# Slabs behind a norm that run unscaled, two-head units in window attention, and modulation rows spread over two layers

## The chip, the cores and the metric

The kernel runs on one core of a Trainium2 chip. The metric is the time of one execution on the device in microseconds (us), all weights read from HBM. The engines are TensorE (PE, its weight loads PEld), VectorE (DVE), ScalarE (ACT), GpSimd (POOL) and SyncE (SP, here only DMA issues). They run their own instruction streams and wait for each other on semaphores.

## What is computed

Two blocks in a row on one sequence of 512 tokens of width 1024, everything in float32. Cut to what matters:

```python
# first block
n = rms_norm(h, attn_norm_w); proj = n @ w_in
y_attn = windowed_gqa_sink(rope(norm(aq)), rope(norm(ak)), av, sink)  # 8 heads, |i-j| <= 128, sink logit in the softmax
y_ret  = silu(rg) * rms_norm(bidirectional_retention(rope(rq), rope(rk), rv))
h = h + concat(y_attn, y_ret) @ w_out
m = rms_norm(h, ffn_norm_w); h = h + (silu(m @ w_gate) * (m @ w_up)) @ w_down
# second block: nine modulation vectors of 1024 from c
mod = silu(c) @ w_ada + b_ada      # sh1 sc1 g1 sh2 sc2 g2 sh3 sc3 g3
u = rms_norm(x) * (1 + sc1) + sh1; x = x + 0.5 * g1 * swiglu(u)
u = rms_norm(x) * (1 + sc2) + sh2; z = u @ w_mix + b_mix   # mLSTM, forgetting attention, gates
x = x + g2 * (merged @ w_out)
u = rms_norm(x) * (1 + sc3) + sh3; x = x + 0.5 * g3 * swiglu(u)
```

## The kernel before

Activations lie transposed: `h`, `xh`, `xl` are 128 partitions by 8 chunks of 512 tokens. A float32 product is made of three matmuls in the reduced type fp32r: high part by high part, high by low and low by high (`slab`, L384). The unit of work is a **slab**: the weights of one output tile of 128 columns, eight blocks of 128x128, so 24 matmuls of 128x512; in a down-projection two slabs of eleven blocks (33 matmuls) make a tile. Slabs are numbered through the program. Slab n is loaded by SP into `raw` (L274, once the `w_lo` of slab n-2 is there), ACT copies it to the high part `whi` (L776, once PE is done with slab n-2), POOL subtracts for the low part `wlo` (L338), and PE runs it. There are two buffers at each place.

The stages in slabs: `att` 6, `ret` 16 in four **mixing steps**, `out` 8, `ff0` 44, `down0` 16, `ff1` 44, `down1` 16, `mlstm` 24, `fox` 24, `merge` 32, `out2` 8, `ff2` 44, `down2` 16. The scheduling is written out by hand in the order of each engine's program.

**Norms.** There are five, r = 0 to 4. While a stage ends, ACT squares each finished chunk of `h` (L804) and DVE adds it to `ssum` (L1250). PE then sums over partitions (`norm_sum`, L395), ACT makes `rstd` by Ln and Exp (L808, L810), DVE scales the chunk by weight and `rstd` (L1263), ACT makes `xh` (L820 to L828), and the low part `xl` comes from DVE for even chunks (L1269) and from POOL for odd ones (L345, `norm_lows`). PE's first slab takes chunk by chunk what is ready.

**Mixing steps.** Each step t does two heads of window attention as eight units of one head and one block of 128 queries: `win_scores` (L436 and L437 are the query-key product, L439 and L441 the masks), the maximum and Exp on DVE and ACT, DVE's scaling (L1414), `win_turn` (L451, transposes of `prob`), `win_values` (L463). Between the units stand pieces of the four `ret` slabs, and at the end the retention of two heads (L480 to L520). ACT moves the ret tiles out of PSUM (`ret_tile` and others). The sink enters by an Exp of its own on ACT (L869) and an addition on DVE (L1410).

**Modulation.** 72 rows of `w_ada` (`adaw`, 128x1024 each) are multiplied by `crow` and summed on DVE (L1534), all beside `ff0`: nine steps of four slabs with eight rows each. In a step DVE makes for each of two tiles the product (`aprod`, L1520), two rows, the low part (L1526), two rows. `adaw` has two buffers.

**Gates.** Behind norm 3 PE first makes the 96 gate rows (L599), and a chain on ACT, DVE, PE and POOL's and ACT's queues leads from them (`zg`, L1013) to the slabs of the mLSTM.

## Time and profile before

| | us |
|---|---|
| median of three runs | 2174.14 (2173.87 to 2176.86) |
| the profiled execution | 2177.48 |
| its span | 2175.7 |
| PE busy | 2048.2 |
| DVE, ACT, POOL busy | 879.9, 771.4, 794.7 |
| the five norms' sums: PE waits for `ssum` | 30.6 |

The span runs from the first instruction to the last; the execution is 1.8 longer. A busy time is the time in which the engine had an instruction under way. The rows that follow further down come from a list of what PE waited for, from the timeline (one row for a group of equal instructions in a row: start, duration, engine, line, operation, what is written and read, count, and in brackets the idle time before and who ended it) and from windows (a stretch of the span with each engine's busy time in it).

### The profile page before, as it was taken

Reading aid. Unit: us, or ns where it says so; the run is one execution under the profiler, and the core shown is the slowest. Engines: PE = TensorE matmul, PEld = TensorE weight load, DVE = VectorE, ACT = ScalarE, POOL = GpSimd, SP = SyncE. Lnnn points to the kernel's source line nnn. Section 1 sums busy time; section 2 is a strip of 40 time slices with the busy share of each in tenths; the row PEclk is TensorE's granted clock in tenths of the full one; section 3 lists DMA queues with packets and bytes.
Section 4 is the critical chain, followed back from the end, with each engine's and each line's share of the span. In section 5 each row is a group of like instructions: output and inputs, shape, how many; then the busy total and the mean of one; then the engine's idle time right before and its main releaser. Section 6 shows DMA issues by size and latency. Waiting matters only on the chain.

```text
span 2175.7 us, 27408 instructions
## 1 busy us (share of the span) xinstructions
PE 2048.2 (94%) x9306; PEld 1603.5 (74%) x9306; DVE 879.9 (40%) x1215; ACT 771.4 (35%) x1197; POOL 794.7 (37%) x322
## 2 busy tenths in 40 slices
PE   5988898888899899999989999999999998999999
PEld 3666676677778778888866776677688886888887
DVE  6556555555542232222236555444421244222200
ACT  4433333222222242222225455555532224222221
POOL 3211134333344344444433233122234444444443
PEclk9999999999999989999999999999999998999999
DMA  4111113777632223333221122111123332333332
GB/s 132 58 39 39 39 58 126 241 233 237 232 126 93 91 68 96 96 96 109 93 79 53 63 67 68 49 51 55 59 78 96 96 97 68 96 96 96 107 101 92
DMA packets 56630, 210.57 MB, mean 97 GB/s; under 512 B 6288, under 2 KB 7056, under 8 KB 56592
## 3 DMA queue, kind: packets, MB, share of 16 engines
q1 hardware_dynamic: 55440, 208.71, 30.1%
q10 hardware_dynamic: 1152, 1.38, 0.2%
q8 instruction: 21, 0.34, 0.1%
q14 instruction: 17, 0.14, 0.0%
HBM read 207.96 MB, written 2.10 MB: 97 GB/s over the span
## 4 chain that ended last, share of the span: by engine, by line
PE 69%; issue 15%; DMA 7%; DVE 4%; POOL 2%; ACT 2%; DVEq 0%; ACTq 0%; SPq 0%; POOLq 0%
PE bank L384 62%; DMA adaw<-ada_dram 7%; POOL wlo L338 2%; DVE adaw L1534 2%; PE bank L617 1%; PE bank L672 1%; PE bank L687 1%; PE bank L698 1%; PE bank L707 1%; DVE sqn L1263 1%; DVE ssum L1250 1%; POOL xl L345 1%; DVE xl L1269 0%; PE bank L395 0%; PE bank L408 0%
## 5 line engine op out<-in xcount | busy, mean ns | idle before, releaser
L338 POOL TENSOR_TENSOR wlo<-raw,whi 128x1024 fp32r<-128x1024 f32 (+1 forms) x298 | 762.7, 2560 | 1320.9 <-ACT whi L776 1320.9
L384 PE MATMUL bank<-xh,whi 128*128 128x512 f32 x1744 | 715.3, 410 | 54.4 <-DVE aprod L1520 25.9
L384 PE MATMUL bank<-xh,wlo 128*128 128x512 f32 x1744 | 689.9, 396 | 0.0
L384 PE MATMUL bank<-xl,whi 128*128 128x512 f32 x1744 | 689.4, 395 | 0.0
L776 ACT ACTIVATE whi<-raw 128x1024 fp32r<-128x1024 f32 (+1 forms) x298 | 330.4, 1109 | 655.9 <-PE bank L384 624.8
L384 PEld LDWEIGHTS bank<-xh,whi 128*128 128x128 f32 x1744 | 334.1, 192 | 150.9 <-issue 68.8
L384 PEld LDWEIGHTS bank<-xl,whi 128*128 128x128 f32 x1744 | 334.9, 192 | 72.2 <-issue 7.4
L384 PEld LDWEIGHTS bank<-xh,wlo 128*128 128x128 f32 x1744 | 333.4, 191 | 72.1
L384 PE MATMUL bank<-acth,whi 128*128 128x512 f32 x528 | 205.6, 389 | 0.1
L384 PE MATMUL bank<-actl,whi 128*128 128x512 f32 x528 | 205.4, 389 | 0.0
L384 PE MATMUL bank<-acth,wlo 128*128 128x512 f32 x528 | 205.4, 389 | 0.0
L1520 DVE TENSOR_TENSOR aprod<-bank,gsil 128x512 f32<-128x512 f32 x66 | 45.5, 689 | 335.7 <-PE bank L384 335.7
L1534 DVE SCALAR_TENSOR_TENSOR adaw<-adaw,crow 128x1024 f32<-128x1024 f32 x72 | 114.7, 1602 | 103.3 <-DMA adaw<-ada_dram 103.3
L1526 DVE TENSOR_TENSOR actl<-aprod,acth 128x512 f32 x66 | 123.1, 1865 | 45.6 <-ACT acth L993 45.6
L384 PEld LDWEIGHTS bank<-acth,whi 128*128 128x128 f32 x528 | 99.1, 188 | 21.7 <-issue 1.2
L384 PEld LDWEIGHTS bank<-acth,wlo 128*128 128x128 f32 x528 | 99.1, 188 | 20.7
L384 PEld LDWEIGHTS bank<-actl,whi 128*128 128x128 f32 x528 | 99.1, 188 | 20.4
L1250 DVE TENSOR_TENSOR ssum<-ssum,sqn 128x512 f32<-128x512 f32 x40 | 93.3, 2334 | 36.2 <-ACT sqn L804 35.5
L988 ACT ACTIVATE gsil<-bank 128x512 f32<-128x512 f32 x66 | 39.1, 593 | 173.1 <-PE bank L384 173.0
L1502 DVE SCALAR_TENSOR_TENSOR h<-bank,gat,h 128x512 f32 x24 | 18.0, 751 | 199.8 <-PE bank L384 199.8
L1396 DVE TENSOR_REDUCE stat<-bank 128x1 f32<-128x256 f32 (+3 forms) x96 | 47.1, 491 | 118.1 <-PE bank L679 64.8
L993 ACT ACTIVATE acth<-aprod 128x512 f32 (+1 forms) x66 | 41.6, 630 | 102.5 <-DVE aprod L1520 102.5
(287 smaller groups left out, 1871.9 us busy)
## 6 DMA issues: line engine op xcount, KB each, us to landing
raw<-w_dram SPq DMA_DIRECT2D x250, 512.0 KB, 3.6
adaw<-ada_dram SPq DMA_DIRECT2D x72, 512.0 KB, 4.2
raw<-wd_dram SPq DMA_DIRECT2D x48, 704.0 KB, 4.0
h<-x_dram SPq DMA_DIRECT2D x4, 512.0 KB, 5.7
out_dram<-h SPq DMA_DIRECT2D x8, 256.0 KB, 4.3
rel<-rel_dram ACTq DMA_DIRECT2D x1, 513.0 KB, 5.0
crow<-c_dram SPq DMA_DIRECT2D x1, 512.0 KB, 3.3
gates_raw<-gates_dram SPq DMA_DIRECT2D x1, 384.0 KB, 8.8
```

The lines of the kernel that those rows point to most:

```text
L338: nc.gpsimd.tensor_tensor(wlo[:, s, 0:width], raw[:, s, 0:width], whi[:, s, 0:width].bitcast(F32), ALU.subtract).then_inc(sem("w_lo"), 1)
L345: nc.gpsimd.tensor_tensor(xl[:, c, :], tmp[c % 3], xh[:, c, :].bitcast(F32), ALU.subtract).then_inc(sem("x_lo1"), 1)
L384: mm = nc.tensor.matmul(proj[b][:], w[:, s, W], v[:, k, :], start=first and j == 0 and a == 0, stop=last and j == len(chunks) - 1 and a == ...
L617: mm = nc.tensor.matmul(bank[5 + j][:, b * P:S], w, sT[:, b % 2, 0:S - b * P], start=b == 0, stop=b == NB - 1, skip_group_check=True)
L776: nc.scalar.activation(whi[:, s, 0:width], raw[:, s, 0:width], ACT.Copy).then_inc(sem("w_hi"), 1)
L988: nc.scalar.activation(gsil[:, jj, :], proj[0][:], ACT.Silu).then_inc(sem("evac0"), 1)
L993: nc.scalar.activation(chunk(acth, j), aprod[:, jj, :], ACT.Copy).then_inc(sem("act_hi"), 1)
L1250: V.tensor_tensor(ssum[:], ssum[:], sqn[:, k, :], ALU.add).then_inc(sem("ssum"), 1)
L1396: V.tensor_reduce(st[:, 0:1], bank[2 + k % 2][:, 0:width], AX.X, ALU.max).then_inc(sem("rowmax"), 1)
L1520: V.tensor_tensor(aprod[:, jj, :], proj[1][:], gsil[:, jj, :], ALU.mult).then_inc(sem("evac1"), 1)
L1526: V.tensor_tensor(chunk(actl, j), aprod[:, jj, :], chunk(acth, j).bitcast(F32), ALU.subtract).then_inc(sem("act_lo"), 1)
L1534: V.scalar_tensor_tensor(W, W, 1.0, crow[:], ALU.mult, ALU.mult, accum_out=modc[:, bass.ds(v * KC + k, 1)]).then_inc(sem("ada_acc"), 1)
```

## The change

1. *Norms.* In the step before a norm, ACT also writes the chunk times the norm's weight, without `rstd`, to `xh` (`z_high`) and DVE its low part to `xl` (`z_low`). The first two slabs behind norms 1, 2 and 4, and the first slab and the gates behind norm 3, run on these; `norm_sum` stands before the fourth chunk of the first of them. The result is multiplied by `rstd` on leaving PSUM (`ff_first`, `gates_scaled`). For r of 2 to 4 the shift is added through two matmuls of 128x2 per chunk (`shs`) and a small sum on DVE (`shift_column`). Chunk by chunk, as the second of the two frees them, `xh` and `xl` are written properly scaled for all further slabs. POOL now makes two of the low parts, chunks 1 and 3, with a `wlo` behind each. Behind norm 0 all of `att` and `ret` runs unscaled, and DVE takes the factor in when it moves a tile out of PSUM (`att_scaled`, `ret_tile`; this was ACT's).
2. *Start.* SP loads the columns, weights and input in another order; ACT issues the constants' loads after the sixth chunk.
3. *Window attention.* Units of two heads: the query-key product in F32 with the two heads in the two halves of the rows (L498), the sink as one more column by a matmul with one column (L505), the values of both heads in turns (L528). DVE no longer splits queries and keys. Its order in a step is changed; `ret_queries` stands ahead of the second rope.
4. *Modulation rows.* Four per step: 28 beside `ff0` (7 steps), 44 beside `ff1` (11 steps). SP issues the rows of a step beside the weights of the step after it, those of the last step in a loop of their own ahead of `down1`.

```diff
+            def load_x(c):
+                sp.dma_start(h[:, c * 2 * S:(c + 1) * 2 * S], x_in[:, c * 2 * S:(c + 1) * 2 * S]).then_inc(sem(f"x_in{c}"), 16)
+
+            sp.dma_start(col[:], cols_in).then_inc(sem("cols_in"), 16)
+            load_wide(None, 2, 0, 0)
+            load_x(0)
+            load_x(1)
+            load_wide(None, 2, 0, 1)
+            load_x(2)
+            load_x(3)
             sp.dma_start(gates_raw[:], gates_in).then_inc(sem("gates_in"), 16)
...
+            def load_ada(i, r0, s):
+                sp.wait_ge(sem("ada_acc"), primed(i * 4 + (r0 + max(s - 1, 0))))
+                sp.dma_start(adaw[:, s % 2, :], ada_in[bass.ds(i * 4 + (r0 + s), 1)].rearrange("a p n -> (a p) n")
+                             ).then_inc(sem(f"ada_in{s % 2}"), 16)
+
+            with sp.Fori(0, ADA0) as i:
                 for s in range(4):
                     load_wide(i, 4, SLAB["ff0"] + 4, s)
-                    for k in range(2 * s, 2 * s + 2):
-
-                        sp.wait_ge(sem("ada_acc"), primed(i * KC + max(k - 1, 0)))
-                        sp.dma_start(adaw[:, k % 2, :], ada_in[bass.ds(i * KC + k, 1)].rearrange("a p n -> (a p) n")
-                                     ).then_inc(sem(f"ada_in{k % 2}"), 16)
-            wide_loop(SLAB["ff0"] + 4 * (NMOD + 1), (N_FF - 4 * (NMOD + 1)) // 2)
+                    load_ada(i, 0, s)
+            wide_loop(SLAB["ff0"] + 4 * (ADA0 + 1), (N_FF - 4 * (ADA0 + 1)) // 2)
             down_loop(0)
-            wide_loop(SLAB["ff1"], N_FF // 2)
+            for s in range(4):
+                load_wide(None, 4, SLAB["ff1"], s)
+            with sp.Fori(0, FC // 2 - 1) as i:
+                for s in range(4):
+                    load_wide(i, 4, SLAB["ff1"] + 4, s)
+                    load_ada(i, 4 * ADA0, s)
+            with sp.Fori(0, 1) as i:
+                for s in range(4):
+                    load_ada(i, 4 * ADA0 + 4 * (FC // 2 - 1), s)
             down_loop(1)
...
             def norm_lows(r):
 
-                for c in range(1, KC, 2):
-                    pool.wait_ge(sem("x_hi"), KC * r + c + 1)
-                    nc.gpsimd.tensor_tensor(xl[:, c, :], tmp[c % 3], xh[:, c, :].bitcast(F32),
-                                            ALU.subtract).then_inc(sem("x_lo1"), 1)
-
-
-            low_loop(0, 2, WC)
-            norm_lows(0)
-            low_loop(2, SLAB["ff0"], WC)
+                n = SLAB[FIRST[r]] + 2
+                norm_low(r, 1)
+                low(n, 0)
+                norm_low(r, 3)
+                low(n + 1, 1)
...
-                nc.tensor.matmul(bank[4][:], ones[:], ssum[:], start=True, stop=True).then_inc(sem("norm_sum"), 1)
+                nc.tensor.matmul(bank[6][:], ones[:], ssum[:], start=True, stop=True).then_inc(sem("norm_sum"), 1)
+
+            def unscaled(r, hi, lo, dst, at, j, done, rows=P):
+
+                for k in range(KC):
+                    if j == 0:
+                        pe.wait_ge(sem("z_lo"), primed(KC * r + k + 1))
+                        if k == 3:
+                            norm_sum(r)
+                            if r > 1:
+                                pe.wait_ge(sem("shifts"), r - 1)
+                    if r > 1:
+                        for a, w in enumerate((hi, lo)):
+                            nc.tensor.matmul(bank[5][0:rows, at:at + 2], w(k), shs[:, r - 2, k, :], start=k == 0 and a == 0,
+                                             stop=k == KC - 1 and a == 1, skip_group_check=True)
+                    for a, (w, v) in enumerate(((hi, xh), (hi, xl), (lo, xh))):
+                        mm = nc.tensor.matmul(dst, w(k), v[:, k, :], start=k == 0 and a == 0, stop=k == KC - 1 and a == 2,
+                                              skip_group_check=True)
+                    if k == KC - 1:
+                        mm.then_inc(sem(done), 1)
+                    elif j == 1:
+                        mm.then_inc(sem("z_used"), 1)
...
+            def win_scores(t, b):
+
                 lo, hi = keys(b)
-                H = slice(e * DH, e * DH + DH)
-                if k == 0:
-                    pe.wait_ge(sem("q_low"), t * 2 + 2)
-                if k >= 2:
-                    pe.wait_ge(sem("probs"), t * 8 + (k - 1))
-                elif not isinstance(t, int) or t > 0:
-                    pe.wait_ge(sem("ret_decayed"), t * 2 + (k - 1))
-                dst = bank[2 + k % 2]
-                W = window(k)
-                B, C = slice(b * P, (b + 1) * P), slice(lo * P, (hi + 1) * P)
-
-                nc.tensor.matmul(dst[:, 0:W], wqs[:, e, B], wks[:, e, C], start=True, stop=False, skip_group_check=True)
-                mm = nc.tensor.matmul(dst[:, 0:W], wqs[H, e, B], wkl[H, C], start=False, stop=False, skip_group_check=True)
+                W = window(2 * b)
                 if b > 0:
-                    mm = nc.tensor.matmul(dst[:, 0:P], identb[:], geb[:], start=False, stop=b == NB - 1, skip_group_check=True)
-                if b < NB - 1:
-                    mm = nc.tensor.matmul(dst[:, W - P:W], identb[:], leb[:], start=False, stop=True, skip_group_check=True)
-                mm.then_inc(sem("scores"), 1)
+                    pe.wait_ge(sem("probs"), t * 8 + 2 * b)
+                elif t == 0:
+                    pe.wait_ge(sem("rope_out"), primed(2))
+                else:
+                    pe.wait_ge(sem("ret_decayed"), t * 2)
+                C = slice(lo * P, (hi + 1) * P)
+                for e in range(2):
+                    H = slice(e * DH, e * DH + DH)
+                    nc.tensor.matmul(bank[2 + e][:, 0:W], qall[H, t, b * P:(b + 1) * P], kf[H, C], start=True, stop=False, skip_group_check=True)
+                for e in range(2):
+                    dst = bank[2 + e]
+                    if b > 0:
+                        nc.tensor.matmul(dst[:, 0:P], identb[:], geb[:], start=False, stop=b == NB - 1, skip_group_check=True)
+                    if b < NB - 1:
+                        nc.tensor.matmul(dst[:, W - P:W], identb[:], leb[:], start=False, stop=True, skip_group_check=True)
+                    nc.tensor.matmul(dst[:, W:W + 1], ident[:], c1("sink", t + e * (AH // 2)), start=True, stop=True,
+                                     skip_group_check=True).then_inc(sem("scores"), 1)
...
+                for b in range(NB):
+                    win_turn(t, 2 * b)
+                    win_turn(t, 2 * b + 1)
+                    if b + 1 < NB:
+                        win_scores(t, b + 1)
+                    if b == 1:
+                        wide("ret", t, 4, 1, part=(0, 3))
+                        ret_turn(t, 0)
+                        wide("ret", t, 4, 1, part=(3, 6))
+                    else:
+                        for j, lo, hi in RET_BESIDE[b]:
+                            wide("ret", t, 4, j, part=(lo, hi))
+                    if b == 2:
+                        ret_turn(t, 1)
+                    win_values(t, b)
...
+            def ff_tiles(run):
+                for j in range(2):
+                    unscaled_slab(NORM[run], j, bank[2 + j][:], 2 * j, j)
+                for s in range(2, 4):
+                    ff_slab(run, 0, s)
...
+            def z_high(r, m, weight):
+
+                nc.scalar.activation(chunk(xh, m), chunk(h, m), ACT.Identity, scale=weight(m)).then_inc(sem("z_hi"), 1)
+
+            def norm(r, shift=None, splits={}):
+
+                inverse_root("norm", r, bank[6][:], rstd[:], D)
+                    if c in splits:
+                        split(0, 2, SLAB[FIRST[r]] + 2, splits[c], WC)
...
+            def z_low(r, m, weight):
+
+                dve.wait_ge(sem("z_hi"), m + (KC * r + 1))
+                V.scalar_tensor_tensor(chunk(xl, m), chunk(h, m), weight(m), chunk(xh, m).bitcast(F32), ALU.mult,
+                                       ALU.subtract).then_inc(sem("z_lo"), 1)
...
-                for c in range(0, KC, 2):
-                    low(c)
-                    for d in (c + 3, c + 4):
-                        if d < KC:
-                            scaled(d)
+                low(0)
+                scaled(3)
+                scaled(4)
+                low(2)
+                scaled(5)
+                low(4)
+                if beside:
+                    beside()
+                scaled(6)
+                low(5)
+                scaled(7)
+                low(6)
+                low(7)
...
+            def ret_tile(t, j):
+                matmuls(t * 4 + (SLAB["ret"] + j + 1))
+                if j < 2:
+                    V.scalar_tensor_tensor(rraw[:, j, :], proj[j][:], DH ** -0.5 if j else 1.0, rstd[:], ALU.mult,
+                                           ALU.mult).then_inc(sem(f"evac{j}"), 1)
+                else:
+                    V.tensor_tensor((vraw, rsil)[j - 2][:], proj[j - 2][:], rstd[:], ALU.mult).then_inc(sem(f"evac{j - 2}"), 1)
...
+            def ff_first(run):
+                n = SLAB[f"ff{run}"]
+                matmuls(n + 1)
+                V.tensor_tensor(aprod[:, 1, :], bank[2][:], rstd[:], ALU.mult).then_inc(sem("evac0"), 1)
+                if run > 0:
+                    shift_column(0, 0)
+                matmuls(n + 2)
+                V.tensor_tensor(aprod[:, 0, :], bank[3][:], rstd[:], ALU.mult).then_inc(sem("evac1"), 1)
+                if run > 0:
+                    shift_column(2, 1)
+                    dve.wait_ge(sem("z_bias"), (0, 2, 6)[run])
+                dve.wait_ge(sem("evac1"), primed(TILE[f"ff{run}"] // 2 + 1))
+                dve.wait_ge(sem("ff_sil"), run + 1)
+                V.scalar_tensor_tensor(aprod[:, 0, :], aprod[:, 0, :], fb[:, 1:2] if run > 0 else 0.0, gsil[:, 0, :], ALU.add,
+                                       ALU.mult).then_inc(sem("ff_first"), 1)
...
+            def ff_beside_ada(run, i, r0, i0):
 
                 for jj in range(2):
-                    ff_product(0, i, i0, jj)
-                    ada_parts(v, range(4 * jj, 4 * jj + 2))
-                    ff_low(0, i, i0, jj)
-                    ada_parts(v, range(4 * jj + 2, 4 * jj + 4))
+                    if i0 or jj:
+                        ff_product(run, i, i0, jj)
+                    else:
+                        ff_first(run)
+                    ada_part(i, r0, 2 * jj)
+                    ff_low(run, i, i0, jj)
+                    ada_part(i, r0, 2 * jj + 1)
...```

How it moves instructions, at the three places that matter most. PE's stream at the start of `ff1` (`xh`, `xl` activations, `shs` the shift, `z_lo` and `x_lo0`, `x_lo1` the semaphores of low parts), before:

```order
L384 MATMUL bank<-acth,wlo 128x512
L398 REGISTER_ALU
L398 COMPARE_AND_BRANCH
L395 MATMUL bank<-ssum,ones 128x512 [waits ssum]
L589 UNCONDITIONAL_BRANCH
L589 ISA
L375 ISA [waits w_lo]
L384 MATMUL bank<-xh,whi 128x512 [waits x_lo0,evac0]
L384 MATMUL bank<-xl,whi 128x512
```

and after, from the third chunk of the first slab on:

```order
L447 MATMUL bank<-shs,whi 128x2 [waits z_lo]
L447 MATMUL bank<-shs,wlo 128x2
L450 MATMUL bank<-xh,whi 128x512
L450 MATMUL bank<-xl,whi 128x512
L450 MATMUL bank<-xh,wlo 128x512
L434 MATMUL bank<-ssum,ones 128x512 [waits ssum,z_lo]
L447 MATMUL bank<-shs,whi 128x2 [waits shifts]
L447 MATMUL bank<-shs,wlo 128x2
L450 MATMUL bank<-xh,whi 128x512
```

The sum has moved from ahead of the slab to its fourth chunk, and two small matmuls stand ahead of each three. POOL's stream at the same norm, before:

```order
L345 TENSOR_TENSOR xl<-sqn,xh 128x512 [waits x_hi] x2
L345 TENSOR_TENSOR xl<-ssum,xh 128x512 [waits x_hi]
L345 TENSOR_TENSOR xl<-sqn,xh 128x512 [waits x_hi]
L334 UNCONDITIONAL_BRANCH
L334 ISA
L338 TENSOR_TENSOR wlo<-raw,whi 128x1024 [waits w_hi]
```

and after:

```order
L379 TENSOR_TENSOR xl<-sqn,xh 128x512 [waits x_hi]
L373 TENSOR_TENSOR wlo<-raw,whi 128x1024 [waits w_hi]
L379 TENSOR_TENSOR xl<-sqn,xh 128x512 [waits x_hi]
L373 TENSOR_TENSOR wlo<-raw,whi 128x1024 [waits w_hi]
L364 UNCONDITIONAL_BRANCH
```

Two weights' low parts have moved between and behind the two activations' that are left. SP's stream at the end of `ff1`, before:

```order
L274 ISA [waits w_lo]
L274 DMA raw<-w_dram 128x1024
L285 REGISTER_ALU
L285 COMPARE_AND_BRANCH
L291 UNCONDITIONAL_BRANCH
L291 ISA
L274 ISA [waits w_lo]
L274 DMA raw<-wd_dram 128x1408
```

and after:

```order
L286 DMA raw<-w_dram 128x1024
L330 REGISTER_ALU
L331 ISA [waits ada_acc]
L331 DMA adaw<-ada_dram 128x1024
L342 REGISTER_ALU
L342 COMPARE_AND_BRANCH
L346 UNCONDITIONAL_BRANCH
L331 DMA adaw<-ada_dram 128x1024 [waits ada_acc] x4
L346 REGISTER_ALU
L346 COMPARE_AND_BRANCH
L303 UNCONDITIONAL_BRANCH
L303 ISA
```

Four rows of `adaw`, each with a wait for DVE's products, now stand between the last slab of `ff1` and the first of `down1`.

## Rows read from the trace of the kernel before

**Rows 1.** The page, busy us, share of the span, instructions.

```profile
PE 2048.2 (94%) x9306; PEld 1603.5 (74%) x9306; DVE 879.9 (40%) x1215; ACT 771.4 (35%) x1197; POOL 794.7 (37%) x322
```

**Rows 2.** Windows: stretch, length, busy PE PEld DVE ACT POOL, clock, DMA share, GB/s.

```profile
73.78:128.77 54.99, 49.12 (x262) 34.50 (x263) 33.53 (x73) 21.38 (x51) 12.19 (x5) 0.94 0.16 48
...
338.80:359.10 20.30, 10.87 (x28) 6.01 (x28) 13.85 (x14) 11.41 (x15) 8.58 (x5) 0.75 0.22 77
359.10:633.60 274.50, 248.43 (x1033) 198.98 (x1032) 144.09 (x186) 67.84 (x87) 109.15 (x43) 0.96 0.66 219
...
753.40:775.30 21.90, 12.38 (x28) 7.31 (x28) 13.55 (x14) 13.49 (x18) 8.75 (x5) 0.61 0.08 24
775.30:1009.40 234.10, 234.06 (x1033) 193.51 (x1032) 62.53 (x42) 68.83 (x86) 103.77 (x43) 1.00 0.31 96
```

**Rows 3.** What PE waited for: us in total, times, longest.

```profile
PE bank L395 <- DVE ssum L1250: 30.6, 5, 13.9
PE bank L384 <- DVE aprod L1520: 25.9, 12, 3.5
...
PE bank L451 <- DVE prob L1414: 6.9, 8, 1.1
PE bank L499 <- DVE kz L1346: 6.3, 4, 1.7
```

**Rows 4.** Timeline at norm 2.

```profile
754.80 2.34 POOL L338 TENSOR_TENSOR wlo<-raw,whi 128x1024 fp32r<-128x1024 f32 x1 [5.08 <-ACT whi L776]
...
755.28 2.41 DVE L1250 TENSOR_TENSOR ssum<-ssum,sqn 128x512 f32<-128x512 f32 x1 [0.85 <-ACT sqn L804]
757.74 2.07 PE L395 MATMUL bank<-ssum,ones 128*128 128x512 f32 x2 [4.17 <-DVE ssum L1250]
...
764.12 0.77 PE L384 MATMUL bank<-xh,whi 128*128 128x512 f32 x1 [4.31 <-DVE xl L1269]
```

**Rows 5.** Timeline at the start.

```profile
7.48 6.26 DVE L1250 TENSOR_TENSOR ssum<-ssum,sqn 128x512 f32<-128x512 f32 x8 [5.08 <-ACT sqn L804]
...
24.41 0.77 PE L384 MATMUL bank<-xh,whi 128*128 128x512 f32 x1 [8.47 <-DVE xl L1269]
...
34.72 0.40 PE L384 MATMUL bank<-xh,whi 128*128 128x512 f32 x1
```

**Rows 6.** Timeline, small matmuls of the mixing steps and of the forgetting attention.

```profile
82.17 0.87 PE L463 MATMUL bank<-pT,vtok 128*64 128x128 f32 x6
...
93.99 0.42 PE L436 MATMUL bank<-wks,wqs 128*128 128x384 f32 x1
...
94.72 0.23 PE L439 MATMUL bank<-geb,identb 128*128 128x128 bf16 x1
...
107.25 0.66 PE L480 MATMUL bank<-ident,rkf 128*128 128x128 f32 x4
...
1429.04 0.92 PE L672 MATMUL bank<-fk,fq 64*128 64x384 f32 x4
1429.50 0.64 PE L676 MATMUL bank<-fsp,selp 64*128 64x384 f32 x2
...
1443.91 0.88 PE L698 MATMUL bank<-fpT,fv 128*64 128x128 f32 x12
```

**Rows 7.** Timeline from the gates to the second slab of the mLSTM.

```profile
1151.08 0.69 ACT L1013 ACTIVATE zg<-bank,col 96x512 f32<-96x512 f32 x1 [2.60 <-PE bank L599]
...
1170.13 0.80 PE L384 MATMUL bank<-xh,whi 128*128 128x512 f32 x1 [2.77 <-POOL wlo L338]
```

**Rows 8.** The page's DMA issues, groups by form, and one load in ff0.

```profile
raw<-wd_dram SPq DMA_DIRECT2D x48, 704.0 KB, 4.0
...
L776 ACT ACTIVATE whi<-raw 128x1408 fp32r<-128x1408 f32 x48 | 66.3, 1382 | 260.1 <-PE bank L384 260.1
...
L338 POOL TENSOR_TENSOR wlo<-raw,whi 128x1408 fp32r<-128x1408 f32 x48 | 154.5, 3220 | 196.5 <-ACT whi L776 196.5
...
368.45 0.33 SPq L274 DMA_DIRECT2D raw<-w_dram  x1
```

More of the change, by code:

```diff
@@ L164, in build @@
         ry = sb("ry", [P, S], F32, abs_)
-        kf = ry
+        kf = sb("kf", [P, S], F32, abs_)
         abs_.close()
@@ L653, in mlstm_head @@
                 wide("mlstm", hd, 6, 7, part=(6, KC))
-            for s in range(2):
-                wide("mlstm", 0, 6, s)
+            slab(SLAB["mlstm"] + 1, 1, 1, (TILE["mlstm"] + 1) // 2, xh, xl, range(KC), ready=("x_lo", 3))
             with pe.Fori(0, MH) as hd:
@@ new lines, in _ @@
+            FF_SPLITS = {0: 0, KC - 1: 1}
+            steps("out", 2, N_OUT // 2, out_step(1, "out", scale_of(1)), "ff0")
+            norm(1, splits=FF_SPLITS)
+            ff_steps(0, "down0")
+            steps("down0", 4, N_DOWN // 4, down_step(2, "down0", scale_of(2)), "ff1")
+            norm(2, shift=0, splits=FF_SPLITS)
+            ff_steps(1, "down1")
+            steps("down1", 4, N_DOWN // 4, down_step(3, "down1", scale_of(3)), "mlstm")
+            norm(3, shift=3, splits={0: 0})
```

476 lines of the change are left out of this document (255 added, 221 removed).

## The prediction

> **What bounds the kernel now.** I read the page's totals first. TensorE is busy for 94% of the span [rows 1], so a gain must be a stretch in which PE waits, runs slowly, or does work it need not do. The windows by stage come next [rows 2]. The stretch 775.3 to 1009.4 is the second feed-forward layer behind its first slab: 43 slabs in 234.1 us, 5.44 us each, at granted clock 1.00. The stretch 359.1 to 633.6 is the same work in the first layer, 43 slabs in 274.5 us, with DMA at 219 GB/s. The two stretches around a norm (338.8 and 753.4) hold one slab each and last 20.3 and 21.9 us. One mixing step lasts 54.99 us, of which PE is busy 49.12. Third, the list of PE's waits [rows 3]: `ssum` (the norms' sum of squares) 30.6 us, `aprod` 25.9, `prob` 6.9, `kz` 6.3. So there are three costs that a change can take: the norms, the modulation rows beside the first layer, and the mixing steps. One execution gives all durations: 2177.5 us, 3.3 above the median of the runs, 2174.1. I sum against the first and take 3.3 off.
>
> **Modulation rows, +40.4.** Eight rows per step of four slabs make 8 x 0.5 MB plus 4 x 0.5 MB in about 25.6 us; DVE then gets the rows late, `aprod` late, PE waits. The whole loss is the difference of the two rows of [rows 2]: 274.5 - 234.1 = 40.4, waits of 25.9 and slowed matmuls (clock 0.96) together. Four rows per step need 4 MB in 21.8 us, 193 GB/s, less than the 219 that the queue carried on the average of that stretch. For DVE, four rows are half of what a step held. I take the loss of a four-row step as zero in both layers; it is bounded by 0 below and by what an eight-row step loses, 40.4 / 9 = 4.5, above.
>
> **The end of ff1, -10.5.** SP loads the rows of a step one step late, and the last four rows have a loop of their own ahead of the down-projection's weights. Counted from the start of slab 41 of 44: PE needs the first down slab after three slabs, at 16.35. The fourth row's load waits for DVE's product of the row two before, which stands behind the products of slab 43, at about 13.5; the weight load follows at 14.1, where it now goes out about 3.8 after a slab's start [rows 8]. From there: 4.0 to 4.5 for 704 KB, 1.4 for the ScalarE split, 3.22 for POOL's remainder [rows 8], so ready at 23.4. PE stands for 7.0 us. A stretch after such a wait ran at clock 0.61 to 0.75 [rows 2]; a slab at half clock costs up to 7.5 more, and I take half of it, 3.5. Bounds -5 (two rows ready early) and -14.
>
> **Norms 1, 2 and 4, +4.4.** Take norm 2 [rows 4]. Now: last square added 757.69, `ssum` product to 759.8, slab 0 from 764.12 chunk by chunk, slab 1 done at 780.7 (775.3 plus 5.45). After: chunks 0 to 2 of slab 0 run from 753.4, PE waits for `ssum` (about 1.4), product 2.07, five chunks, then slab 1. The 16 tiny matmuls per slab for the shift cost at least a weight load each, 0.147 (0.66 / 4, the row of L480 in [rows 6]), so 2.35 per slab. Slab 1 is done near 772.5: 8.2 ahead. What is late next is slab 2, the first on the properly scaled activations. Its eight chunks still need VectorE's scaling and remainders, and POOL now has two weight remainders of 2.3 us between its two chunk remainders. DVE and POOL take turns: a DVE add of two SBUF operands took 2.41 us beside a POOL operation and ended 0.55 after it [rows 4]. ScalarE's split for slab 4 stands behind the table load and the first product. I place slab 4's start at 788.9 against 791.6. That gives 2.7 for norms 2 and 4, and 3.5 for norm 1, which has no shift. From this goes the clock: the slabs behind the wait were slow because they waited, and now run bare at a clock of 0.61 to 0.75 at first; one slab at half clock costs 5.45, and I take 1.5 per norm. Sum 8.9 - 4.5 = 4.4, bounds -8 (a slab cold per norm) and +24 (three times 8).
>
> What the row shows is that DVE does not share with POOL but waits until it ends. The Trainium skill (SBUF — State Buffer, section "SBUF: two separate sides") says the pair of ports is locked for a whole instruction by whichever comes first, which speaks against giving POOL more between the chunks; a model of sharing would bring the norm gain near its upper bound.
>
> **Norm 3, -5.** The chain that ends with the mLSTM's first recurrence starts at the gates' evacuation, 1151.08, and reaches PE 19.05 later at 1170.13 [rows 7]. The evacuation now comes behind the norm's last `x_hi`, and DVE puts three operations on slab 0's product ahead of the row work: +5.6, less 2 for less contention, and 1.4 of clock. Bounds -8 and +1.
>
> **Start, +5.** Now PE starts slab 0 at 24.41 and ends it at 34.7 [rows 5]. After, it waits first for weights: issued near 3, load 4.0, split about 1.0 (1.38 x 1024 / 1408), remainder 2.34 [rows 4, 8], so 10.3. Then for eight chunks on DVE, a square added at 0.78 (6.26 / 8 in [rows 5]) and a `z_low` of about the same each, 1.6, behind a ScalarE that has splits and DMA issues between: the last near 23, and product and last chunk end near 27, 7.7 earlier. Two to three of these go again at the end of the attention projections, where `vraw` is now evacuated by DVE behind a rope. Bounds 0 and 11.
>
> **Mixing steps, +26.** For two heads at 384 keys the fp32r pair of matmuls takes 2 x 0.73 = 1.46 us (93.99 to 94.72); the forgetting attention's F32 pair of heads takes 0.46 (1429.04 to 1429.50) [rows 6]. That is 1.0 per unit, 0.9 at 256: 3.8 per step. Values of one head take 0.87 us busy for six matmuls, twelve interleaved ones of two heads 0.88 [rows 6]; with the overlap at the ends 0.8 per unit, and 0.6 at 256: 2.8 per step. Eight one-column sink matmuls cost one to two weight loads of 0.147 each plus a change of type: 1.2 to 3.6; I take 2.6. Net 4.0 of PE work per step. The `kz` wait (6.3 / 4 = 1.6) goes, since the queries' part is moved ahead of the second rope; half of the `prob` waits (6.9 / 4 / 2 = 0.9) goes, since a pair has twice the matmuls to hide behind. 4.0 + 1.6 + 0.9 = 6.5, times four is 26. DVE is busy 33.5 of 55 us [rows 2]; it loses the query split and gains four evacuations of about 0.7, so I leave it off the path. Bounds 12 (two-head softmax chain of twice the length shows once per step, 3.5) and 34.
>
> The rows of L672 and L676 leave 0.46 between them for both heads [rows 6]. The Trainium skill (FP8 and Floating Point Precision, section "TensorE Precision Notes") says true FP32 takes four passes; if the heads did not overlap that would be eight passes of 384 columns per unit.
>
> **Sum.** 40.4 - 10.5 + 4.4 - 5 + 5 + 26 = 60.3. 2177.5 - 60.3 = 2117.2; less 3.3: **2114**.
>
> **Rivals.**
> 1. *The norms gain in full.* DVE and POOL keep up and slab 4 starts behind slab 1 at once, since now the same eight chunks of scaling end by 775.3 without anything to cover them; three times 8.2 less 2.7 to 3.5 is 15.7: 2098. Against: DVE's stretched rows [rows 4]. 0.18.
> 2. *No bare wait at the end of ff1.* DVE has little to do there, and the last rows could be done before slab 43: +10.5, 2104. 0.10.
> 3. *DVE becomes the bound of a mixing step.* The evacuations stand in its order behind softmax work and behind POOL's turns, so the split slabs wait for their bank. A step gains 1 instead of 6.5: +22, 2136. For it: DVE's turns with POOL, as at 755.28 [rows 4]; against: 61% busy [rows 2]. 0.15.
> 4. *F32 scores without overlap.* At 0.227 per pass of 512 columns (5.45 / 24), 0.17 for 384, eight are 1.36 against 1.46 now: the 3.8 per step is 0.4, 13.6 less gain, 2128. This is the skill's rule without the row. 0.04.
> 5. *Slower.* Each of 18 four-row steps, 7 in ff0 and 11 in ff1, loses as much as an eight-row step now, 4.5 us, because what hurts is a row product between the product and its remainder on DVE and not the bandwidth. 18 x 4.5 = 81 on top of 2114: 2195. It decides from 3.4 us a step (60.3 / 18). 0.04, of it 0.01 near that point.
>
> The forecast itself has 0.49. The change surely does what it says, as the order of instructions shows the pairs, the rows and the tiny matmuls.
>
> **How the numbers follow.** The likeliest case gives 2114. Its unknown terms (norms -12 to +20, mixing -14 to +8, end of ff1, start, each about 5) together move it some 20 either way. Rivals 1 and 2 lie at 2098 and 2104, rival 3 at 2136, so 2088 to 2146 leaves out rival 5 and the far ends, under 0.2 in all. A measurement of this kernel tells 0.2% (4.3 us) from no change. Faster by more: all but rival 5, 0.96; within 0.01; slower 0.03.
>
> **What the profile after would show.** ff0 and ff1 behind their first slabs at 234 us each with no `aprod` wait; a hole of about 7 us before the first matmul of the second down-projection, released by POOL's `wlo`; the stretch from the last down matmul to slab 4 of ff1 shorter by about 3 us, with PE's waits on `xl` in slab 2 and `wlo` in slab 4; mixing steps near 48.5 us; the gates' evacuation 5 us later after T0. Wrong would be: waits in slab 2 of zero (rival 1), a mixing step over 52 us with PE waiting on DVE's evacuations (rival 3), four-row steps above 22.5 us (rival 5).

## The result, and the profile after

| | before | after |
|---|---|---|
| median of the runs, us | 2175.5 (2173.9 to 2179.4) | 2117.3 (2116.9 to 2117.7) |
| span of the profiled execution | 2175.7 | 2115.8 |
| ratio, 95% interval | | 0.973 (0.9713 to 0.9747) |

The forecast was 2114 with a range of 2088 to 2146. The spans differ by 59.9 us where 60.3 were forecast. That the sums agree to 0.4 us is luck: the gains were 16 us larger than forecast, and 16 us were lost in a place that the prediction did not look at.

The page after, against [rows 1] (busy us, share, instructions):

```profile
PE 2036.8 (96%) x9466; PEld 1598.8 (76%) x9466; DVE 863.2 (41%) x1242; ACT 772.8 (37%) x1176; POOL 770.7 (36%) x310
```

PE is busy 11.4 us less and idle 48.5 less. What it waited for, against [rows 3]:

```profile
PE bank L423 <- DVE xl L1357: 13.5, 4, 11.2
PE bank L423 <- DVE xl L1372: 11.7, 15, 1.8
PE bank L619 <- ACT rsq L1005: 11.7, 4, 3.1
PE bank L423 <- POOL wlo L373: 11.3, 2, 10.3
PE bank L423 <- POOL wlo L368: 8.0, 2, 7.1
PE bank L434 <- DVE ssum L1347: 7.1, 5, 2.2
...
PE bank L515 <- DVE prob L1517: 0.9, 1, 0.9
```

`ssum` fell from 30.6 to 7.1, though part of that moved: before, 13.9 of the 30.6 were waited for the first sum of the program, and now 11.2 of the first row stand ahead of its first chunk. `aprod` (25.9) and `kz` (6.3) are gone. The two rows of `wlo` are new in size: their longest waits are 10.3 and 7.1 us, where waits for `wlo` came to 3.7 in all before. Windows of after, against [rows 2] (the same columns): a mixing step, ff0 from its slab 4, most of down0, ff1 from its slab 4:

```profile
117.20:164.42 47.22, 44.01 (x279) 32.48 (x278) 28.69 (x63) 18.09 (x37) 9.74 (x4) 0.97 0.13 45
...
338.60:556.40 217.80, 217.79 (x962) 180.04 (x960) 77.74 (x92) 64.07 (x80) 96.52 (x40) 1.00 0.48 161
556.40:676.20 119.80, 119.80 (x514) 96.55 (x515) 37.59 (x29) 31.49 (x32) 50.85 (x16) 1.00 0.29 93
...
713.83:931.30 217.47, 217.47 (x961) 179.99 (x959) 84.49 (x122) 62.85 (x79) 93.29 (x39) 1.00 0.58 194
```

Forty slabs of ff0 and forty of ff1 take 217.8 and 217.5 us, 5.44 each, at clock 1.00: four rows per step cost nothing. The third row is where the time went that nobody counted. 514 matmuls in 119.8 us of down0, with PE never idle and at clock 1.00; the kernel before had 529 in as long:

```profile
633.60:753.40 119.80, 119.79 (x529) 99.00 (x528) 33.00 (x24) 25.94 (x24) 50.71 (x16) 1.00 0.30 98
```

The table follows the first matmul of each stage in both timelines. Gains are positive. The last row is worked out: the slabs of these stages times what one takes longer. The rows for the norms are without it.

| stretch | forecast | measured |
|---|---|---|
| start, to the first transposes of the mixing steps (73.8 against 66.5) | +5 | +7.3 |
| four mixing steps (218.2 against 191.4) | +26 | +26.8 |
| norms 1, 2, 4, to slab 4 behind each | +4.4 | +4.1 +4.1 +3.5 = +11.7 |
| rows beside ff0 | +40.4 | +40.4 |
| end of ff1 and first down slab | -10.5 | -8.7 |
| norm 3, to slab 4 of the mLSTM | -5 | -1.4 |
| out, the down-projections, merge, out2: slower matmuls | 0 | -15.9 |

### The profile page after: what moved, and what is told of

Read it like the earlier page. It is cut to its first block, busy times and chain, and to the rows that moved or that the text cites. A ratio compares the mean times of both kernels' runs of the same rounds, so it can differ in the third digit from the quotient of the medians.

```text
span 2115.8 us, 27569 instructions
## 1 busy us (share of the span) xinstructions
PE 2036.8 (96%) x9466; PEld 1598.8 (76%) x9466; DVE 863.2 (41%) x1242; ACT 772.8 (37%) x1176; POOL 770.7 (36%) x310
## 4 chain that ended last, share of the span: by engine, by line
PE 70%; issue 22%; POOL 5%; DVE 2%; ACT 1%; POOLq 0%; ACTq 0%; DVEq 0%
PE bank L423 62%; POOL wlo L368 4%; PE bank L686 1%; PE bank L740 1%; PE bank L755 1%; PE bank L766 1%; PE bank L450 1%; PE bank L775 1%; DVE xl L1372 0%; DVE ssum L1347 0%; DVE sqn L1366 0%; POOL wlo L373 0%; PE bank L472 0%; POOL xl L379 0%; PE bank L747 0%
## 5 line engine op out<-in xcount | busy, mean ns | idle before, releaser
L368 POOL TENSOR_TENSOR wlo<-raw,whi 128x1024 fp32r<-128x1024 f32 (+1 forms) x290 | 738.6, 2547 | 1260.5 <-ACT whi L842 1260.5
L423 PE MATMUL bank<-xh,whi 128*128 128x512 f32 x1688 | 684.4, 405 | 36.5 <-DVE xl L1357 13.5
L423 PE MATMUL bank<-xh,wlo 128*128 128x512 f32 x1688 | 663.0, 393 | 0.0
L423 PE MATMUL bank<-xl,whi 128*128 128x512 f32 x1688 | 662.8, 393 | 0.0
L423 PEld LDWEIGHTS bank<-xh,whi 128*128 128x128 f32 x1688 | 320.3, 190 | 119.1 <-issue 19.6
L423 PEld LDWEIGHTS bank<-xl,whi 128*128 128x128 f32 x1688 | 320.4, 190 | 69.4 <-issue 7.0
L423 PEld LDWEIGHTS bank<-xh,wlo 128*128 128x128 f32 x1688 | 319.8, 189 | 68.6
L423 PE MATMUL bank<-acth,whi 128*128 128x512 f32 x528 | 209.8, 397 | 7.1 <-POOL wlo L368 7.1
L423 PE MATMUL bank<-actl,whi 128*128 128x512 f32 x528 | 209.4, 397 | 0.0
L423 PE MATMUL bank<-acth,wlo 128*128 128x512 f32 x528 | 209.3, 396 | 0.0
L423 PEld LDWEIGHTS bank<-acth,whi 128*128 128x128 f32 x528 | 99.6, 189 | 32.3 <-issue 8.3
L423 PEld LDWEIGHTS bank<-acth,wlo 128*128 128x128 f32 x528 | 99.6, 189 | 24.1
L423 PEld LDWEIGHTS bank<-actl,whi 128*128 128x128 f32 x528 | 99.7, 189 | 23.9
L1657 DVE TENSOR_TENSOR actl<-aprod,acth 128x512 f32 (+1 forms) x66 | 94.0, 1425 | 32.5 <-ACT acth L1061 30.8
L1347 DVE TENSOR_TENSOR ssum<-ssum,sqn 128x512 f32<-128x512 f32 x40 | 92.8, 2321 | 30.4 <-ACT sqn L870 30.4
L1504 DVE TENSOR_REDUCE stat<-bank 128x1 f32<-128x257 f32 (+5 forms) x96 | 47.2, 491 | 101.2 <-PE bank L747 64.3
L1928 DVE TENSOR_TENSOR br<-bank,sg 128x512 f32<-128x512 f32 x15 | 10.4, 692 | 122.0 <-PE bank L423 122.0
## 6 DMA issues: line engine op xcount, KB each, us to landing
raw<-wd_dram SPq DMA_DIRECT2D x48, 704.0 KB, 4.1
```

What stands on the lines that cost most here:

```text
L368: nc.gpsimd.tensor_tensor(wlo[:, s, 0:width], raw[:, s, 0:width], whi[:, s, 0:width].bitcast(F32), ALU.subtract).then_inc(sem("w_lo"), 1)
L423: mm = nc.tensor.matmul(proj[b][:], w[:, s, W], v[:, k, :], start=first and j == 0 and a == 0, stop=last and j == len(chunks) - 1 and a == ...
L1347: V.tensor_tensor(ssum[:], ssum[:], sqn[:, k, :], ALU.add).then_inc(sem("ssum"), 1)
L1504: V.tensor_reduce(st[:, 0:1], bank[2 + k % 2][:, 0:width], AX.X, ALU.max).then_inc(sem("rowmax"), 1)
L1657: V.tensor_tensor(chunk(actl, j), aprod[:, jj, :], chunk(acth, j).bitcast(F32), ALU.subtract).then_inc(sem("act_lo"), 1)
```

## The experiments

**Where the 15.9 us went.** A slab of a down-projection (33 matmuls) takes 7.48 us before and 7.70 after, one of out2 5.44 and 5.60, and slabs on `xh` and `xl` take 5.44 in both. The intervals are even, 0.227 and 0.233 us. What the slow ones share is where their activations lie: `acth`, `yh`, `yah`, `mgh` and the rest are allocated behind the new small buffer `fb`. Its 16 bytes a partition take 32 in the allocation, and so these buffers start 32 bytes past a multiple of 64 (`acth` at byte 115552 in the built program); in the kernel before they start at a multiple (115328). The weights `whi` and `wlo` lie ahead of it and start at a multiple in both. The first run moves the activations back.

```diff
-        fb = sb("fb", [P, 4])
+        fb = sb("fb", [P, 16])
```

> The changed kernel with one buffer of 4 columns (fb, 16 bytes a partition) made 16 columns wide, so that all buffers behind it start at a multiple of 64 bytes again, as they did in the kernel before; in the changed kernel they start 32 bytes past one. In the traces a down-projection slab of 33 matmuls takes 7.70 us after and 7.48 before, at granted clock 1.00 in both, a slab of out2 5.60 after and 5.44 before, and slabs that read xh and xl, which lie ahead of that buffer, 5.44 in both. Theory (the start of the moving operand costs the difference): down slabs back at 7.48, merge and out2 at 5.44, 15.9 us less in all (48 x 0.22, 32 x 0.09, 16 x 0.16), 2117.3 to about 2101. Rival (the unrolled mixing steps or the code's place do it): within 2 us of 2117.

Measured: 2099.2 us (2096.8 to 2101.8), ratio to before 0.9651 (0.9633 to 0.967), 18.1 less than after. A window of its second down-projection has 332 matmuls in 75 us:

```profile
975.00:1050.00 75.00, 75.00 (x332) 62.14 (x331) 23.59 (x15) 19.16 (x20) 31.94 (x11) 1.00 0.28 91
```

Down slabs are back at 7.48 and those of merge and out2 at their old pace. Of the 18.1 us the pace explains 15.9. In the traces most of the rest is in `out`: it gave 3.4 where the pace explains 1.3, since it ran at clock 0.95 after and at 1.00 in e1. The mixing steps, which run ahead of `out`, take the same in both. The opposite, on the kernel before:

```diff
         epsc = sb("epsc", [P, 1])
+        sb("pad", [P, 8])
```

> The kernel before with 32 unused bytes a partition allocated ahead of the activation buffers of all stages, and nothing else. Theory of the operand's start: down slabs 7.70, and about 16 us more, 2174 to 2190. Rival (program's shape): no change, 2174.

Measured: 2194.4 us, 1.0082 (1.0058 to 1.0106) times before. The same window there holds 323 matmuls:

```profile
1045.00:1120.00 75.00, 75.00 (x323) 60.24 (x323) 20.32 (x10) 16.40 (x15) 32.30 (x10) 1.00 0.26 90
```

32 unused bytes cost this kernel 20 us (16.7 in the trace) and nothing else of the program differs, so its shape is not what sets the pace. Is it the place of the moving operand (the activations) alone, or does that of the stationary one (the weights) count too? The weights' buffers were shifted next, on the kernel e1:

```diff
+        sb("pad0", [P, 8])
         raw = sb("raw", [P, 2, DC])
...
+        sb("pad1", [P, 8])
         col = sb("col", [P, NCOL])
```

> The aligned kernel (e1) with raw, whi and wlo, the weights' buffers, 32 bytes past a multiple of 64 and all others as in e1. Theory (only the moving operand's start counts): slabs stay at 5.44 and 7.48, time as e1, 2099. Rival (the stationary operand's start counts as well): slabs at 5.5 to 5.6, 30 us or more on top.

Measured: 2143.7 us (one run), 44.5 more. The theory is wrong: all slabs are slow now, 5.60 and 7.70, those on `xh` too. Then everything was shifted, activations and weights alike:

```diff
+        sb("pad0", [P, 8])
         h = sb("h", [P, KC * S])
```

> The aligned kernel (e1) with 32 unused bytes a partition ahead of every buffer, so that activations and weights all start 32 bytes past a multiple of 64. With the activations alone past it (after) a slab of 33 took 7.70, with the weights alone (e7) 7.70 as well. Theory (either operand past the multiple sets the slower pace, once): all slabs 5.60 and 7.70, as e7, 2144. Rival (the two add): 5.76 and 7.92, about 2180. Second rival (only their relative place counts): 5.44 and 7.48, 2099.

Measured: 2101.8 us (one run), and 5.44 and 7.48 again, as the second rival said. Windows of the down-projection with the weights shifted, and with all shifted:

```profile
1000.00:1075.00 75.00, 75.00 (x323) 60.26 (x322) 23.63 (x15) 19.16 (x20) 31.49 (x10) 1.00 0.26 87
```

```profile
978.00:1053.00 75.00, 75.00 (x332) 62.12 (x331) 23.59 (x15) 19.17 (x20) 31.96 (x11) 1.00 0.27 91
```

So it is not that an address is bad. These fp32r matmuls of 128x512 follow each other at 0.227 us when the moving and the stationary operand start at the same place within 64 bytes, and at 0.233 when they are 32 bytes apart. Four arrangements of two offsets gave this without exception. Why the chip does so is not shown here; only offsets of 0 and 32 were tried, and two of the four arrangements in one run each.

**The rows by themselves.** The kernel before with the rows spread and nothing else; SP's loops are those of the change.

```diff
-            with dve.Fori(0, NMOD) as i:
-                ff_beside_ada(i, 0, i)
+            with dve.Fori(0, ADA0) as i:
+                ff_beside_ada(0, i, 0)
...
-            ff_products(1)
+            with dve.Fori(0, FC // 2) as i:
+                ff_beside_ada(1, i, 4 * ADA0)
```

> The kernel before with the modulation rows spread as in the changed kernel (28 beside ff0, 44 beside ff1, four per step, the last four loaded ahead of the second down-projection's weights), and nothing else of the change. Theory of the recorded sum, by its own steps: ff0 40.4 shorter, 8.7 to 10.5 back at the end of ff1: 2174 to about 2143. Rival (part of ff0's gain came with the other parts, or ff1 pays for the rows): 2150 or more.

Measured: 2144.1 us, ratio 0.9858 (0.9826 to 0.989); 30 less than before. In its trace ff0 is 40.4 shorter from slab 4 on, and 8.5 come back from there in ff1 to the second down slab. The term is as forecast, and does not depend on the rest of the change.

**The loads ahead of the second down-projection.** SP's stream in after, and PE's first matmul of down1:

```profile
920.43 7.14 SPq L331 DMA_DIRECT2D adaw<-ada_dram  x4
928.09 14.40 SPq L286 DMA_DIRECT2D raw<-wd_dram  x4
```

```profile
938.67 0.76 PE L423 MATMUL bank<-acth,whi 128*128 128x512 f32 x1 [7.08 <-POOL wlo L368]
```

The wait is 7.08 us where 7.0 was forecast. The slab behind it took 9.25 for 7.58 before, at clock 0.82: 1.7 and not 3.5, and 0.2 of that is the slower pace. The experiment moves loads and nothing else:

```diff
+            for k in range(2):
+                load(SLAB["down1"] + k, k, wd_in[N_DOWN + k], DC)
                 with sp.Fori(0, 1) as i:
-                    for s in range(4):
+                    for s in range(2 * k, 2 * k + 2):
                         load_ada(i, 4 * ADA0 + 4 * (FC // 2 - 1), s)
-            down_loop(1)
+            down_loop(1, 1)
```

> The aligned kernel (e1) with SP's last four row loads put behind the first and the second weight load of the second down-projection, two and two. Theory of the recorded sum: the wait of 7.1 us ahead of that down-projection and the slow clock behind it (1.7) go, 8.8 less than e1, about 2092. Rival (DVE's last row products hold up the low part of the last activation chunk, as PE needs it later anyway): the wait moves to the second down slab, and less than 4 us are gained.

Measured: 2095.1 us, 0.9631 (0.9615 to 0.9647), 4.0 less than e1 by medians (e1's own runs span 5 us). In the traces the place itself gives 8.1: the first down slab starts 6.7 earlier relative to e1, the second another 1.4, and the wait of 7.1 has become 0.46:

```profile
928.04 0.47 PE L425 MATMUL bank<-acth,whi 128*128 128x512 f32 x1 [0.46 <-POOL wlo L370]
```

The traced executions differ by only 3.5, because e3's lost time elsewhere. Ahead of the edit, where the programs do the same, it lost 1.6 in out (clock 0.96 for 1.00), 0.6 before out and 0.6 net at norm 1; the rest lies in pieces under 1 us behind it. So the wait went as forecast, and the medians show half of it.

**The norms: what the unscaled chunks cover.** PE at norm 2 in after, against [rows 4]:

```profile
684.13 1.10 PE L434 MATMUL bank<-ssum,ones 128*128 128x512 f32 x2 [1.56 <-DVE ssum L1347]
...
699.13 0.50 PE L423 MATMUL bank<-xh,whi 128*128 128x512 f32 x1 [0.60 <-DVE xl L1372]
...
706.00 0.50 PE L423 MATMUL bank<-xh,whi 128*128 128x512 f32 x1 [1.80 <-DVE xl L1372]
```

```profile
679.80:689.80 10.00, 8.44 (x46) 6.62 (x44) 5.88 (x6) 3.51 (x5) 2.37 (x1) 1.00 0.15 52
689.80:697.00 7.20, 7.20 (x40) 6.07 (x41) 4.00 (x3) 4.88 (x7) 3.81 (x3) 1.00 0.00 0
697.00:707.10 10.10, 6.98 (x25) 4.30 (x25) 9.70 (x12) 5.41 (x7) 3.94 (x2) 0.97 0.37 111
707.10:713.80 6.70, 6.70 (x25) 5.43 (x24) 4.91 (x7) 2.38 (x4) 2.39 (x1) 0.80 0.38 149
```

The wait for `ssum` is 1.56 (forecast 1.4) where it was 4.17, and the clock stays at 1.00 through slabs 0 and 1. The first real loss is slab 2, 10.2 us, on DVE's chunks. The slow clock that the forecast expected behind `ssum` comes only there: slab 3 takes 6.7 us at clock 0.80. The next run takes the cover away.

```diff
-                        if k == 3:
+                        if k == 0:
                             norm_sum(r)
```

> The aligned kernel (e1) with the norm's sum ahead of the first chunk of the first unscaled slab instead of its fourth (norms 1 to 4). Theory (slab 0, slab 1 and the chunks of slab 2, which are written as PE frees them, stand in series): the three chunks that now cover the wait for ssum are lost, 2.0 us at norm 1 and 2.7 at the others, 10 more than e1 in all, 2109. Rival (slab 2 is bound by the chain from rstd, whose start does not move): under 3 us.

Measured: 2119.1 us, 0.9749 (0.9731 to 0.9767), 19.9 more than e1, twice the theory. At norm 2 PE waits 4.27, the sum takes 2.04 instead of 1.10, and slab 0 behind it runs at 0.79:

```profile
680.76 2.04 PE L434 MATMUL bank<-ssum,ones 128*128 128x512 f32 x2 [4.27 <-DVE ssum L1347]
```

```profile
676.40:682.90 6.50, 2.23 (x6) 1.14 (x5) 3.77 (x3) 2.25 (x4) 2.35 (x1) 0.77 0.25 77
682.90:692.00 9.10, 9.10 (x42) 7.76 (x42) 2.08 (x3) 1.26 (x2) 0.00 (x0) 0.79 0.01 3
```

The lost cover is 2.7; the sum, at the lower of the two clock levels (1.2 for 2.4 GHz), costs 0.9 more, and slab 0, which would take 7.3 (8 x 0.91), takes 9.1. That is 5.4 in these terms, of which 0.8 comes back by slab 4. By the traces e11 loses 3.8, 4.6, 6.4 and 5.3 us at the four norms. Three chunks of work inside the wait save about as much by the clock and what it slows as by their own length.

The length of the wait alone does not settle the clock. At norm 1 PE waits 2.2 us for `ssum` in the changed kernel and in every run built on it except e11. In four traces (after, e1, e7, e12) the clock stayed at 1.00 in the slab around that wait; in six others (e3, e4, e5, e8, e9, e10) it fell, and that slab took about 1.6 us longer. This is one reason why single traces of like kernels differ by a few us. Slab 0 in e4 and in e1:

```profile
303.82:314.28 10.46, 8.21 (x27) 5.82 (x26) 5.86 (x6) 3.51 (x5) 2.36 (x1) 0.84 0.43 150
```

```profile
302.97:311.79 8.82, 6.57 (x28) 4.81 (x27) 5.63 (x6) 3.51 (x5) 2.36 (x1) 1.00 0.56 178
```

**DVE and POOL in turns.** On top of e1, DVE is given all low parts of activations.

```diff
-        POOL_LOW = (1, 3)
+        POOL_LOW = ()
...
-                norm_low(r, 1)
                 low(n, 0)
-                norm_low(r, 3)
                 low(n + 1, 1)
...
                 low(0)
                 scaled(3)
+                low(1)
                 scaled(4)
                 low(2)
                 scaled(5)
+                low(3)
                 low(4)
```

> The aligned kernel (e1) where DVE also makes the low parts of chunks 1 and 3 behind norms 1 to 4, and POOL only the low parts of weights. Theory (DVE and POOL take turns, and slab 2 behind a norm is bound by that): slab 2 in ff0, ff1 and ff2 takes 7 to 8 us instead of 10.2, 2 to 3 us less for each of four norms, 8 to 12 less than e1. Rival (the chain is bound by ScalarE, which waits for PE to free the chunks): within 2 us of e1, since DVE takes 1.5 us more work in the same stretch.

Measured: 2096.6 us, 0.9639 (0.9623 to 0.9656), 2.5 less than e1 where 8 to 12 were expected. Slab 2 is 8.33 instead of 10.35 in ff1 and 8.64 instead of 9.79 in ff2, but 10.06 instead of 10.39 in ff0. To slab 4 the traces show 2.4, 1.5 and 0.7 us less at norms 2, 3 and 4, 4.6 together; at norm 1 and in out this execution ran at a slower clock than e1's. So giving DVE the work pays, against the rival, but less than half of what the theory had. The edit also brings POOL's low parts of the next slabs' weights forward, so it does not show by itself that the turns were the whole cause. The rest of slab 2 is bound by something else. One guess was ScalarE's split of slab 2's weights, which stands ahead of the first chunk. On top of e4 and e3 (the kernel e10 below):

```diff
-            FF_SPLITS = {0: 0, KC - 1: 1}
+            FF_SPLITS = {1: 0, KC - 1: 1}
...
-            norm(3, shift=3, splits={0: 0})
+            norm(3, shift=3, splits={1: 0})
```

> The kernel e10 with ScalarE's split of slab 2's weights behind the norm's first chunk instead of ahead of it (norms 1 to 4). Theory (the chunks' chain ScalarE - VectorE is in series from the moment at which PE frees chunk 0, and the split of 1.06 us delays it): 1 us less per norm, 4 less than e10. Rival (POOL's low part of slab 2's weights, which then comes 0.7 later, holds slab 2 up, or DVE's scaling is the bound): within 1.5 us of e10.

Measured: 2090.2 us (2085.3 to 2091.7) against 2089.6: no difference. Slab 2 of ff1 went from 8.32 to 8.80. What bounds slab 2 beyond that stays open.

**The two heads of a unit.** A unit at 384 keys in the trace of e1:

```profile
78.91 0.92 PE L498 MATMUL bank<-kf,qall 64*128 64x384 f32 x4
79.76 0.23 PE L502 MATMUL bank<-geb,identb 128*128 128x128 bf16 x1
...
79.88 0.33 PE L505 MATMUL bank<-col,ident 128*128 128x1 f32 x2
80.08 0.22 PE L502 MATMUL bank<-geb,identb 128*128 128x128 bf16 x1
```

Each F32 product has two records, so the row of four is the pair of heads. To the next matmul the pair takes 0.85 us, not 0.46, and a sink 0.20. The experiment puts each head's masks and sink behind its own product, so that the products are not neighbours:

```diff
                     nc.tensor.matmul(bank[2 + e][:, 0:W], qall[H, t, b * P:(b + 1) * P], kf[H, C], ...)
-                for e in range(2):
                     dst = bank[2 + e]
```

> The aligned kernel (e1) with the two F32 query-key matmuls of a unit no longer next to each other: each is followed by its head's masks and sink. In the trace of after the adjacent pair took 0.85 us at 384 keys and 0.64 at 256. Theory (the two heads, in the two halves of the rows, overlap when adjacent): apart each takes about 0.65 or more at 384, 0.3 to 0.5 us more per unit, 16 units, 5 to 8 us more than e1, 2104 to 2107. Rival (0.85 is twice 0.43, no overlap): within 2 us of e1.

Measured: 2116.4 us, 0.9733 (0.9706 to 0.9761), 17 more than e1 (15 in the trace). One head alone takes as long as the pair did:

```profile
80.12 0.91 PE L498 MATMUL bank<-kf,qall 64*128 64x384 f32 x2
80.96 0.23 PE L501 MATMUL bank<-geb,identb 128*128 128x128 bf16 x1
```

The two F32 products overlap wholly when they stand next to each other: 0.84 for one, 0.85 for two. Apart, the second product costs 8 x 0.84 at 384 keys and 8 x 0.63 at 256, 11.8 us. In the trace 11.6 of the 15 lie ahead of out, where the units are; 2.2 are in out and 0.6 at norm 1, where the clock was lower than in e1. Without the overlap the scores would have saved nothing: 2 x 0.84 is 1.68 per unit against 1.46 before. That is more than the 1.36 that the fourth rival of the prediction took.

**Norm 3's chain.** PE waits 10.3 us for slab 3 of the mLSTM, because ScalarE splits its weights behind the placing of the gates' rows. With e3 and e4 together, this order was turned round:

```diff
-            place_rows(0, msM, slice(0, MH), "m_rows")
             conv_tile(0, 1, 0, 1)
+            place_rows(0, msM, slice(0, MH), "m_rows")
```

> The kernel e3 (aligned, last rows behind the down-projection's first loads) with DVE making all activation low parts as in e4, and on ScalarE behind norm 3 the evacuation of the mLSTM's second tile with the split of slab 3 ahead of the placing of the gates' rows, for which it now waits 10 us too long. Theory: the wait of PE for slab 3 (10.3 us) goes and about half comes back at the first head's recurrence, since the rows still end at 1092: with 2.5 of e4 about 8 less than e3, 2087. Rival (the rows' chain is what PE waits for in any case): the wait moves whole, 2092 to 2093.

and, as its control, e3 and e4 together with the order as it was:

> The kernel e8 with the order on ScalarE behind norm 3 as in the changed kernel: aligned, last rows behind the first down loads, DVE making all activation low parts. In the traces e8's early evacuation moved PE's wait of 10.3 us from slab 3 to the slabs behind it, 0 to 1 us worse on balance. Theory (the rows' chain is the bound there): 2089 to 2090, as e8 or 1 less. Rival: 2093, the early evacuation was worth what e8 gained over e3 and e4.

Measured, with the order turned and without: 2089.6 us (ratio 0.9603, 0.9576 to 0.963) and 2089.6 us (0.9608, 0.9593 to 0.9622). PE's wait, with the order as in the change and turned:

```profile
PE bank L423 <- POOL wlo L375: 10.3, 1, 10.3
```

```profile
1091.32 0.79 PE L423 MATMUL bank<-xh,whi 128*128 128x512 f32 x1 [9.97 <-POOL wlo L370]
```

It moved one slab on, whole: the second set of rows stands ahead of the next split. The chain of the gates' rows is the bound. Both are 3 us faster than e3 less the 2.5 of e4 would give; most of that is in the traces, where the edit of e4 is worth 4.4 us at norms 2 to 4 of e10 against e3. Either kernel, at 0.960 and 0.961 of before and 28 us under the changed kernel, is the fastest measured here; the simpler is e10.

## Why the prediction was right, step by step

- **Rows:** right in mechanism and size, shown by e6 (30 us by medians, 32 in its trace's stretches, for 29.9 in the sum). The four-row steps lose nothing in either layer, rival 5 is out.
- **End of ff1:** right in the mechanism, and e3 takes the wait away. The 7.08 us came by two errors that cancel: the load went out 13.0 us after slab 41's start (928.09 against 915.1) for 14.1, and took 5.7 to land for 4.0 to 4.5. The clock term was too large, 1.7 for 3.5. Rival 2 is out.
- **Norms 1, 2 and 4:** the direction was right, the size 11.7 for 4.4. What was mis-sized is read best at norm 2. The way from slab 0 to the end of slab 1 took 17.1 us (679.80 to 696.94) for 19.1 (753.4 to 772.5): the sum took 1.10 for 2.07, since the clock was at 1.00, and a pair of shift matmuls 0.23 (0.91 per chunk against 0.68) for twice 0.147. The quotient that the prediction gives for 0.147, 0.66 / 4, is 0.165, so the misreading went the other way. The clock's 1.5 was placed behind the wait for `ssum`; the slow stretch came at slab 3. Slabs 2 and 3 took 16.9, and 16.1 in e11, where the clock was at 1.00 in both, so it cost 0.8 there. The turns of DVE and POOL are there, but slab 2 gains only 0.3 to 2.0 from e4 of the five or so by which it exceeds 5.44. Rival 1, the full gain, lies 8 us beyond the measured terms.
- **Norm 3:** a loss, as forecast, of 1.4 for 5. The gates' evacuation starts 24.3 us behind the last down matmul (1087.72 against 1063.4) where it was 21.7 before, 2.6 later and not 5.6; from there the chain to slab 3 takes 17.7 (to 1105.38) for 19.1. The term that failed is the delay of the evacuation. It stands behind the norm's last `xh`, as forecast. PE made the gates' rows in 6.8 us at clock 1.00 where they took 11.0 at 0.57 before; whether that is what brought the last `xh` forward, no run shows.
- **Start:** +7.3 for +5. Slab 0 was done at 25.9 where 27 was forecast. No experiment takes this part by itself.
- **Mixing steps:** 26.8 for 26. From the first transposes to out, PE's work fell by 16.6 us, 4.2 a step for 4.0, and its waits by 10.1, 2.5 a step for 2.5 (the first two columns behind the stretch are its length and PE's busy time):

```profile
73.78:291.94 218.16, 194.16 (x1042) 139.43 (x1042) 126.78 (x272) 83.95 (x189) 41.40 (x17) 0.95 0.13 39
```

```profile
66.51:257.89 191.38, 177.52 (x1105) 131.21 (x1103) 111.94 (x244) 70.93 (x143) 39.81 (x17) 0.95 0.15 45
```

  Within both, errors cancel. The price of the scores was misread: I took the distance from L672 to L676 [rows 6] for the length of the F32 pair, but the distance between two starts of different kinds is not a length. The same row of [rows 6] gives 0.92 for the group. Next to a bf16 matmul it is 0.85 (e1), so the scores gave 2.4 a step, not 3.8. The sinks cost 1.6, not 2.6. With 2.8 for the values, read and not measured by a run of its own, that is 3.6 of the 4.2; the other 0.6 is not taken apart. Of the waits, `kz` went as forecast, and the `prob` wait fell by 1.5 a step, not 0.9; other waits of before went too (1.2), and a wait of 2.9 instead of 1.5 on `rsq` at each step's end was not foreseen. Rival 3 is out, since a step takes 47.9 on the average (191.4 / 4), and rival 4 is out by e5.
- **The pace of the matmuls:** no step of the prediction looked at where buffers lie. It took a new buffer of 16 bytes to be free, and its price was 15.9 us by the slabs (18 by medians, e1, of which about 2 is the clock in out). Without it the time would have been 2099, in the range but 15 from the forecast.

## What to carry to other kernels

Count the matmuls in a window in which PE is never idle, before and after: 529 against 514 in 119.8 us shows a slower pace that no list of waits and no busy share tells. Where a small buffer is added, keep what lies behind it in step with what it is multiplied by. A sum that comes out right proves its terms only when each is laid beside its own stretch.
